# A state-space mixer's outputs: the sum of two rotated parts taken from GpSimd into TensorE's accumulation

## The reference, cut to what matters

```python
a = exp((lam_re + 1j * lam_im) * dt)              # 64 complex states a group
bu_re = einsum('sgc,gpc->sgp', u, bb_re)          # inputs of the states
bu_im = einsum('sgc,gpc->sgp', u, bb_im)
x[s] = a * x[s-1] + bu[s]                         # complex scan over 256 steps
y = einsum('sgp,gcp->sgc', x_re, c_re) - einsum('sgp,gcp->sgc', x_im, c_im)
y = y + d_skip * h
g = gelu(y);  val, gate = split(g @ w_glu);  out = val * sigmoid(gate)
```

## Time and profile before

| what | us |
|---|---|
| median of three runs | 2932.88 (2929.36 to 2935.04) |
| the profiled execution | 2934.4 |
| its span, first to last instruction | 2932.7 |
| the state-space blocks in it | about 1120 to 1205 |
| TensorE busy | 2886.0 (98%) |
| VectorE, ScalarE, GpSimd busy | 1799.9, 1410.3, 488.9 |

### The profile page before, as it was taken

One profiled execution on the slowest core, in us unless ns is written; L12 is line 12 of the kernel. 1 busy time (PEld: TensorE's weight loads), 2 busy tenths in 40 slices (PEclk: granted clock), 3 DMA queues, 4 the chain that ended last, 5 costly groups with the idle time before them and its releaser, 6 DMA issues.

```text
span 2932.7 us, 42471 instructions
## 1 busy us (share of the span) xinstructions
PE 2886.0 (98%) x16971; PEld 2401.3 (82%) x16971; DVE 1799.9 (61%) x2025; ACT 1410.3 (48%) x1949; POOL 488.9 (17%) x529
## 2 busy tenths in 40 slices
PE   9999999999999999999999999999999999998998
PEld 8888788878888888888888888888788888888787
DVE  5555657755766677555655556556644666765765
ACT  5555545354453447444444434344544444653444
POOL 3000110891000676300100001011100001000000
PEclk9999999999999999999999999999999999999999
DMA  8676588797686897577867768677776667661364
GB/s 261 207 213 182 172 255 238 253 259 228 208 250 227 237 256 227 158 229 230 237 208 222 221 204 241 193 232 220 230 225 191 197 199 247 221 202 61 130 210 165
DMA packets 407296, 626.78 MB, mean 214 GB/s; under 512 B 119977, under 2 KB 138665, under 8 KB 405442
## 3 DMA queue, kind: packets, MB, share of 16 engines
q1 hardware_dynamic: 382592, 546.71, 62.3%
q0 software_dynamic: 16032, 61.43, 7.1%
q10 hardware_dynamic: 8482, 15.97, 1.5%
HBM read 546.96 MB, written 46.14 MB: 202 GB/s over the span
## 4 chain that ended last, share of the span: by engine, by line
PE 90%; DVE 4%; DMA 3%; ACT 2%; SPq 1%; issue 1%; ACTq 0%; POOL 0%; DVEq 0%; POOLq 0%
PE acc L1164 22%; PE acc L1171 22%; PE acc L1165 22%; PE acc L1259 4%; PE acc L1252 4%; PE acc L1253 4%; DMA raw<-in_mlp_w_dram 1%; DVE wL L2743 1%; PE acc L1938 1%; PE acc L1931 1%; PE acc L1932 1%; PE tp L1179 1%; DMA hT<-plane_scratch 1%; ACT wH L1996 1%; PE acc L1515 0%
## 5 line engine op out<-in xcount | busy, mean ns | idle before, releaser
L2743 DVE TENSOR_TENSOR wL<-raw,wH 128x1024 fp32r<-128x1024 f32 (+1 forms) x968 | 1211.9, 1264 | 1001.2 <-ACT wH L1996 998.0
L1996 ACT CAST wH<-raw 128x1024 fp32r<-128x1024 f32 (+1 forms) x968 | 1012.3, 1050 | 1279.3 <-PE acc L1171 894.3
L1164 PE MATMUL acc<-wH,xH 128*128 128x512 f32 (+1 forms) x2208 | 863.1, 391 | 2.2 <-ACT wH L1996 2.1
L1165 PE MATMUL acc<-wH,xL 128*128 128x512 f32 (+1 forms) x2208 | 855.9, 388 | 0.0
L1171 PE MATMUL acc<-wL,xH 128*128 128x512 f32 (+1 forms) x2208 | 587.2, 388 | 1.8 <-DVE wL L2743 1.8
L1164 PEld LDWEIGHTS acc<-wH,xH 128*128 128x128 f32 x2208 | 415.4, 188 | 88.2 <-ACT wH L1996 3.2
L1171 PEld LDWEIGHTS acc<-wL,xH 128*128 128x128 f32 x2208 | 412.7, 188 | 88.3 <-DVE wL L2743 3.1
L1165 PEld LDWEIGHTS acc<-wH,xL 128*128 128x128 f32 x2208 | 415.4, 188 | 83.7 <-issue 0.5
L1164 PE MATMUL acc<-wH,hH 128*128 128x512 f32 x960 | 374.6, 390 | 1.9 <-DVE hL L2804 1.9
L1165 PE MATMUL acc<-wH,hL 128*128 128x512 f32 x960 | 373.6, 389 | 0.0
L1171 PE MATMUL acc<-wL,hH 128*128 128x512 f32 x960 | 256.7, 389 | 0.5 <-DVE wL L2743 0.5
(11 more groups left out here) (563 smaller groups left out, 2466.0 us busy)
## 6 DMA issues: line engine op xcount, KB each, us to landing
raw<-in_mlp_w_dram SPq DMA_DIRECT2D x512, 512.0 KB, 4.6
raw<-in_w_in_dram SPq DMA_DIRECT2D x192, 512.0 KB, 4.4
raw<-in_a_w_in_dram SPq DMA_DIRECT2D x96, 512.0 KB, 4.3
raw<-in_b_w_glu_dram SPq DMA_DIRECT2D x64, 512.0 KB, 3.9
raw<-in_a_w_out_dram SPq DMA_DIRECT2D x32, 512.0 KB, 4.5
raw<-in_w_out_dram SPq DMA_DIRECT2D x32, 512.0 KB, 4.0
plane_scratch<-planes POOLq DMA_DIRECT2D x16, 512.0 KB, 3.6
raw<-in_w_proj_fox_dram SPq DMA_DIRECT2D x16, 512.0 KB, 4.5
```

What stands on the lines that cost most here:

```text
L1164: nc.tensor.matmul(bank, aH[:, k, rows], wH[:, j % SPLIT, u, 0:n], start=k == 0, stop=False)
L1165: nc.tensor.matmul(bank, aL[:, k, rows], wH[:, j % SPLIT, u, 0:n], start=False, stop=False)
L1996: nc.scalar.copy(wH[:, j % SPLIT, :, 0:n], raw[:, j % RAW, :, 0:n]).then_inc(high_done, 1)
L2743: nc.vector.tensor_tensor(wL[:, j % SPLIT, :, 0:n], raw[:, j % RAW, :, 0:n], wH[:, j % SPLIT, :, 0:n].bitcast(F32), ALU.subtract).then_inc ...
```

## The change

GpSimd's sum goes. The two products write straight into `xs`, which now has both parts for each of its two buffers (the tile `zz` goes, `xs` takes its place too), shifted by one chunk and 63 columns long. The wait for the outputs of two blocks before stands ahead of the first product. TensorE multiplies each part with the same weights: five products an output in place of three, and the loop over the two halves g is now the innermost, so that successive products are in two places of the array in turn. The memset clears the first columns of twice as many parts. The marks "x" are gone; TensorE waits for "zs".

```diff
-        pool += [("zc", b), ("zs", b), ("x", b)]
+        pool += [("zc", b), ("zs", b)]
...
-        zz = at("stg", 0, "zz", [P, 2, 2, 4, S5_N])
-        xs = at("stg", 4, "xs", [P, 2, 2, 4, S5_N])
+        xs = at("stg", 0, "xs", [P, 2, 2, 2, 4, S5_N])
...
-                    pool.wait_ge(s_dve, SDVE["z", b, 1])
-                    SPOOL.mark(s_pool, nc.gpsimd.tensor_tensor(zz[:, 0], blocks[:, 2:4], table(0), ALU.mult), "zc", b)
-                    pool.wait_ge(s_act, SACT["n", b])
-                    SPOOL.mark(s_pool, nc.gpsimd.tensor_tensor(zz[:, 1], blocks[:, 1:3], table(1), ALU.mult), "zs", b)
+                    until = slice(0, S5_N - 1)
                     if b >= 2:
                         pool.wait_ge(s_pe, SPE["y", b - 2])
-                    pool.wait_ge(s_pool, SPOOL["zs", b])
-                    SPOOL.mark(s_pool, nc.gpsimd.tensor_tensor(xs[:, n, :, :, 1:], zz[:, 0, :, :, 0:S5_N - 1], zz[:, 1, :, :, 0:S5_N - 1],
-                                                               ALU.add), "x", b)
-                    pool.wait_ge(s_pool, SPOOL["x", b])
+                    pool.wait_ge(s_dve, SDVE["z", b, 1])
+                    SPOOL.mark(s_pool, nc.gpsimd.tensor_tensor(xs[:, n, 0, :, :, 1:], blocks[:, 2:4, :, until], table(0)[:, :, :, until],
+                                                               ALU.mult), "zc", b)
+                    pool.wait_ge(s_act, SACT["n", b])
+                    SPOOL.mark(s_pool, nc.gpsimd.tensor_tensor(xs[:, n, 1, :, :, 1:], blocks[:, 1:3, :, until], table(1)[:, :, :, until],
+                                                               ALU.mult), "zs", b)
+                pool.wait_ge(s_pool, SPOOL["zs", S5_B - 1])
...
-                pe.wait_ge(s_pool, SPOOL["x", b])
+                pe.wait_ge(s_pool, SPOOL["zs", b])
...
-                        for g in range(2):
-                            o = acc[0][g][quad[h], e * 64:(e + 1) * 64]
-                            nc.tensor.matmul(o, ut[quad[g], b % 4, x], Tt[quad[g], S5_HP * h + 2 * b + e], start=True, stop=False)
-                            nc.tensor.matmul(o, xs[quad[g], b % 2, 0, x], ft[quad[g], b % 3, x, 0], start=False, stop=False)
-                            last = nc.tensor.matmul(o, xs[quad[g], b % 2, 1, x], ft[quad[g], b % 3, x, 1], start=False, stop=True)
+                        for n in range(5):
+                            for g in range(2):
+                                o = acc[0][g][quad[h], e * 64:(e + 1) * 64]
+                                if n == 0:
+                                    nc.tensor.matmul(o, ut[quad[g], b % 4, x], Tt[quad[g], S5_HP * h + 2 * b + e], start=True, stop=False)
+                                else:
+                                    r, part = (n - 1) // 2, (n - 1) % 2
+                                    last = nc.tensor.matmul(o, xs[quad[g], b % 2, part, r, x], ft[quad[g], b % 3, x, r],
+                                                            start=False, stop=n == 4)
...
-            nc.vector.memset(xs[:, :, :, :, 0:1], 0.0).then_inc(s_clear, 1)
+            nc.vector.memset(xs[:, :, :, :, :, 0:1], 0.0).then_inc(s_clear, 1)
```

## The result

Twenty runs of each kernel: 2937.74 us for the changed one, 2932.93 for the one before, a ratio of 1.0016 with a 95% interval of 1.0009 to 1.0023, that is 4.7 us more (2.6 to 6.7). The forecast was 12.8 more, its range began at 2940. Much of the spread between executions of one kernel goes with the mean granted clock of TensorE: of 35 executions of the kernel before that stood beside E5 to E8, the twelve at 0.999 took 2926.7 to 2931.9 us, the four at 0.996 took 2937.2 to 2942.6. The profiled execution of the changed kernel happened to be a short one: 2933.92 us, span 2932.2.

What follows compares the result with a forecast made beforehand. It took TensorE to bound the kernel, GpSimd being off the path; 16 blocks of outputs at +0.80 us gave +12.8, all other parts about 0. From the median 2932.88 that made 2945.7 us, range 2940 to 2951.

Steps and rivals of the forecast that it cites:

- What bounds the loop: State-space blocks: the chain outputs, copy of `ut`, input transposes, states sets the 3.95 us period; GpSimd isn't in it.
- The outputs' length: TensorE's outputs: 80 rows instead of 48 a block, 1.72 to about 2.5 us, +0.80 in each of 16 blocks, +12.8 us.
- the nearest row: The states' rows on TensorE, same tile, sizes and turn, taken as measure for the outputs: 2.54 us a block.
- The order: Outputs with two places in turn: can save at most 0.13 us a block, already in the estimate, so nothing beyond the 0.80.
- rule of strict program order: Outputs: if matmuls start and end in program order, the change saves 0.2 us a block, 2929.7 us; set aside, 1%.
- a part is absorbed: Rival: TensorE's idle 0.61 us before input transposes in every second block swallows part; +8.0 us, 2940.9; 14%.
- The doubled rate: Rival, outputs: two places in turn run rows twice as fast, 1.36 us a block, -6 us, 2927; 4%.
- GpSimd's moved wait: GpSimd's wait for the outputs of two blocks before, now ahead of the first product: four microseconds in hand, cost 0.
- loads: Loads of `ft`, `gt`, `rt`: same number and buffers, longest landing 8.3 us against 10.1 available, 0 us.
- memset: Clearing of the first columns on VectorE doubles from 16 to 32 elements: at most another 0.07 us.
- what follows: After the state-space stretch TensorE is busy 15.00 of 15 us: nothing gives the time back and nothing takes more.

Runs made afterwards that it cites:

- E5: Kernel before without GpSimd's sum, three products in the old order, sine part left out of the outputs: 2933.07 against 2932.65 us, ratio 1.0000.
- E8: The changed kernel measured once more, beside the kernel before on the same chip: 2939.97 against 2932.65 us, ratio 1.002.
- E1: Changed kernel with its five products in the old order, all of one half g, then all of the other: 2963.81 us against 2935.74 for the kernel before.
- E2: Kernel before with its three products in the new order, two places in turn, GpSimd's sum kept: 2933.68 against 2935.74 us, ratio 0.9992.
- E4: Changed kernel with four places in turn, the column half h also inside the loop over products: 2936.87 us against 2935.74 for the kernel before.
- E6: Changed kernel with GpSimd summing the imaginary half, four products an output, four places in turn: 2933.54 us against 2932.65 for the kernel before.
- E7: Changed kernel with four places in turn, tables loaded for the first blocks only and used again: 2925.65 us against 2932.65 for the kernel before.
- E10: Changed kernel with tables loaded for the first three or four blocks only: 2939.87 us against 2942.19 for the kernel before, ratio 1.0011.
- E9: Kernel before with three products in turn, GpSimd's next first product ahead of its sum, two buffers: 2939.78 against 2942.19 us, ratio 1.0000.
- E3: Changed kernel with three products in turn, no sum, sine part left out of the outputs: 2925.19 us against 2935.74 for the kernel before.

## Why the prediction was wrong, point by point

**What bounds the loop: right.** The chain through the copy of `ut`, and GpSimd off it (E5: no change from taking the sum away).

**The outputs' length: the step that failed.** The prediction put "80 x 0.0285 + 0.22 (length of the last row) = 2.50 us", and from the states 2.54, "+0.78 to +0.82; I take +0.80". It is 2.02, +0.31, so the term of +12.8 is +5.0. The reading behind it was wrong: "So each place takes a row every 0.057, and both are fed." Each place takes a row every 0.058 while it works, but it doesn't always work. The 0.0285 was no pace of the array; it was that of handing over from chain to chain: six rows less three that wait are 3 x 0.057 = 0.17 us, and 0.17 / 6 is 0.0285. Chains of ten rows begin every 0.40 us in the old order (E1), pairs of such chains every 0.41 in the new one: again when about three rows of the present chain are left in a place. In the new order the next pair is in the other column half, so all four places work where two pairs overlap, and 20 rows cost 0.41. The states sit in two places for good, each with a row every 0.058, so their 0.029 was no rate for the outputs: "the nearest row" had the same tile and the same turn, and not the change of place. A model of three waiting rows a place gave 3.6, 1.1, 1.45 and 1.2 us before E1, E2, E4 and E6 ran; measured are 3.57, 1.10, 1.39 and 1.16 (the last two need only that places are independent). That it is a line of three by design is not shown, only that it counts so for these rows. Nor is it shown that the three belong to the place and not to the output tile: in every order that was run, a chain of the outputs changes both together.

**The order: wrong.** "So nothing beyond the 0.80" stands against 1.55 us a block between E1 and the changed kernel, 25 us in all. Both edits are of this size: two more products in the old order cost +27 us, and the new order gives back 22. The Trainium skill's rule of strict program order ("TensorE: Matmul & The Clock Gate", Part 3), which the prediction had set aside, would, by an estimate from this trace's rows, have the blocks in the old order at 80 x 0.057 = 4.6 us and those in turn at 2.5; E1 has 3.57, the changed kernel 2.02. The runs agree with it in that the order decides. They don't agree that starts keep to program order: the rows by `ft` at 1142.41 belong to earlier outputs than those by `Tt` at 1142.39.

**The rivals.** That a part is absorbed would have brought the time near the measured one for another reason, and it is not what happened: the outputs grew by 0.31 us, the period by 0.29, and TensorE's wait for the copy of `ut` stayed at 3.7 us, six times 0.6. The doubled rate "decides from 0.019 us a row on"; two places in turn took 0.023, and only four in turn 1.39 / 80 = 0.017 (E4). The Trainium skill ("TensorE: Matmul & The Clock Gate", section "Wait — 56ns, not 53.3ns?") has start to start never below about 25 ns. This is not kept as a mean here: 1.81 us from the first start to the last of 80 rows is 0.023.

**GpSimd's moved wait, loads, memset, what follows: right**, each at nothing. No wait on GpSimd appeared, the memset took 0.085 us, and TensorE was as full after the stretch (583.4 of 585 us from 1215 to 1800, 584.0 before).

**What was missed: TensorE's instructions.** No part of the prediction had a price for feeding it 64 instructions more a block (32 matmuls, 32 weight loads). The gaps are 2.4 and 3.4 us in two profiles of the changed kernel, none over 0.16 in the one before or in E5, and they shrink when the loads go (E7, E10). With them the stretch grew by 7.3 and 8.1 us; the runs as a whole by 4.7 (2.6 to 6.7). That the two differ is left open. One execution of each is compared with the median of twenty, and the rest of a run varies by as much: the profiled pair has nearly the same time (2934.4 and 2933.92), because outside the stretch the changed kernel's was some 8 us shorter. Of that 2.7 us lie ahead of the first outputs (1133.4 against 1136.1), and 6.8 us at the lower clock (from 2075) stand against 3.4 (from 2656). What makes a fetch begin late is open too: that it begins later with the table loads beside it was seen (E10), not how.

No version was shown to beat both. E4, E6 and E9 stand within their intervals of the kernel before, E6 with the reserve about the clock. E7 and E3 show what lies there, -8 and -12 us, with work left out: four places in turn need a cheaper supply of instructions, three products in turn need a sum that isn't on GpSimd.

## What to carry to other kernels

Small products in different places of the array overlap across a change of place only for the last few rows of a chain, so put the loop over places inside the loop over the terms of a sum; here that was worth more than two fifths of the length of the same 80 rows. A rate read from one pattern of places holds for that pattern alone. And when two engines show the same period, take the work off the one and look at what the other does before trading work between them: here the sum was free where it was, and moving it cost.

## What the runs showed of the hardware that was not expected

- Four places of 64 x 64 run fp32 rows side by side, also two column halves over the same rows of the array: 80 rows in 1.39 us, against 2.02 with two in turn and 3.57 one after the other.
- TensorE stalls for its own instructions: gaps of 0.2 to 2.1 us in runs of equal products, each of which ended 2.2 to 2.8 us after the start of a 16 KB fetch. The sum of the gaps was 0 at 3.95 us a block with 48 rows of outputs, 0.2 at 5.8 with 80 rows (E1), 2.4 to 3.4 at 4.24 with 80 rows too, 3.1 and 5.7 where blocks of 80 and 64 rows without gaps take 3.6 and 3.4. With few loads beside it, it was 1.0 (E7) and 0 (E10).
- A stretch of 6.8 us at the lower clock fell among the outputs in the profiles of E4, E6 and E9, and cost up to 2.5 us there. A comparison of stretches between single profiles has to look at the granted clock of each first.
